# Order of the row groups and of the opening block pairs in the seven-product gated blocks

## The chip, the cores and the metric

The kernel runs on one core of one Trainium2 chip. The metric is the device time of one execution in microseconds. A profiled execution has a span (first to last instruction) and a total time slightly above it.

## The reference, cut to what matters

Two transformer blocks, one behind the other, over x of 512 tokens by 1024 features, in float32. The second has two layers, each with two gated feed-forward blocks, four in all:

```
D_MODEL = 1024; SEQ = 512; D_FF_2 = 2816
def swiglu(h, wg, wu, wd):
    return (jax.nn.silu(h @ wg) * (h @ wu)) @ wd
...
    h = modulated_norm(x, norm_g[l, 0], sh1, sc1)
    x = x + 0.5 * g1 * swiglu(h, ffn_wg[l, 0], ffn_wu[l, 0], ffn_wd[l, 0])
    ...   # attention with pooling (layer 0) or short convolution (layer 1)
    x = x + 0.5 * g3 * swiglu(h, ffn_wg[l, 1], ffn_wu[l, 1], ffn_wd[l, 1])
```

## The kernel before, in words

The five engines run five programs written by hand. Each has its own order, and semaphores tie them together; an engine never passes an instruction that waits. Every float32 operand is held as a rounded high part and a low remainder, and every product is three matmuls: high by high, high by low, low by high. ScalarE makes the high part of a piece of weights (a copy into a rounded type), VectorE the low part (raw minus high).

**Groups.** The 2816 hidden columns of a gated block are 22 chunks of 128. `GROUPS` (lines 92 to 96) divides them into 8, 8 and 6. For each group the kernel first makes the hidden rows, two chunks at a time (a block pair: two chunks of gate weights in raw slot 0, two chunks of up weights in raw slot 1, 1024 KB each, loaded by the SP queue), and then multiplies them by the group's rows of the down weights: four units of two output chunks, each unit a sum over the group's chunks (`down`). Behind a unit VectorE adds its result, times a gate, to the residual `xT` (`residual`, line 2359). The last group's last unit is `product_tail`: its second output chunk is made in two token halves, and after three k of the second half TensorE puts in the partial sums of the next norm. The norm's rstd and the first normed rows (ScalarE, line 1534) follow from these sums, and `first_products` (line 818) starts on them.

**Seven products.** In three of the four gated blocks (`SEVEN`; the fourth, layer 0's first, has plain products throughout) the two first pairs of group 0 are plain and all other pairs, nine in each block, are made by seven block products in place of eight: the weights and the activations are cut into 2 by 2 blocks, sums of blocks are multiplied, and the results are combined. This is done for gate (g) and up (u). The weight blocks come in seven batches:

- batch 1 (gate) and 2 (up): two blocks each, straight from the raw slots;
- sums made by VectorE in place, for each of g and u, in the order s3, s2, s4, s1 (`block_sum`, line 2917, 128x512 each; s2 is written into `stats`);
- batch 3: the two s2 sums; batch 4 and 5: s3 and s1 of gate and of up; batch 6 and 7: the rest of gate and of up. The low part of batch 6 frees raw slot 0 and that of batch 7 raw slot 1 for the next load.

`block_hi` (ScalarE, line 1913) and `block_lo` (VectorE, line 2893) split a batch. Batches 4, 5 and 6 live in `x_hi`/`x_lo`, the others in `w_hi`/`w_lo`. TensorE multiplies in the order p1g, p2g, p1u, p2u, p6g, (batch 4), p6u, p7g, (batch 5), p7u, p4g, (batch 6), p4u, (batch 7): 14 block products of 12 matmuls 128x256 (`block_product`, lines 1121 to 1123). p1g of the next pair waits for silu21, p1u for mul21, and p4u for u3u:

```
                else:
                    pe.wait_ge(s_y_act, y_act.after("silu21", w - 1))
                block_product(first_bank(0), 1, 0, *b11, start=True).then_inc(s_y_pe, y_pe.one("p1g"))
...
                else:
                    pe.wait_ge(s_y_dve, y_dve.after("mul21", w - 1))
                block_product(first_bank(1), 2, 0, *b11, start=True).then_inc(s_y_pe, y_pe.one("p1u"))
...
                pe.wait_ge(s_y_act, y_act.after("u3u", w))
                block_product(first_bank(1), 7, 1, *t4).then_inc(s_y_pe, y_pe.one("p4u"))
```

**Taking a pair's results.** `seven_taken` exists for ScalarE and for VectorE. ScalarE copies partial results out of the accumulators (`kept`, line 1955: u1g, u1u, u2g, u2u, u3g, u3u), takes the silus (lines 1986, 1992, 1996) and, between them, splits the batches of the next pair (`ahead`). VectorE adds the blocks: first block (line 2995), fourth block (line 3001, which needs u3), second block (line 3007), then the products mul21 (line 3056), mul22 and mul1; between them it makes the next pair's low parts (`lo`) and sums (`total`).

**Heads.** The first seven-product pair of a group is its head; the head of group 0 (pair 2) is the opening pair. The batches of a head are made ahead by `opening_blocks` and `seven_group`. For a later group this happens in the residual of the down product before it: behind the third unit (v == 2) batch 1, the sums, batches 2, 4, 6; behind the fourth (v == 3) batch 3. Before the change a later head has its four up sums there too, and its batches 5 and 7 stand ahead on ScalarE and just behind first block g on VectorE; the opening pair makes s4u, s1u and batches 5 and 7 inside `seven_taken`. p1g and p1u of a head wait for the residual updates of the units before (`out_taken`).

Of the kernel before, what the change touches and what calls it, by code (L numbers as in the profile page):

```python
# [51 lines left out]
def hybrid_two_block_kernel(  # L52
# [37 lines left out]
    u = U_FF + 8 * FFG  # L90

    GROUPS = []
    left = FF2 // P
    while left:
        GROUPS.append(min(8, left))
        left -= GROUPS[-1]
    U_FFN = {}
    U_AB = U_ABO = U_C = U_CO = 0
    for l in range(2):
        for j in range(2):  # L100
            if j == 1:
                if l == 0:
                    U_AB, U_ABO, u = u, u + 8, u + 12
# [24 lines left out]
    with ctx:  # L128
# [1363 lines left out]
        def _(act):  # L1492
# [448 lines left out]
            def seven_taken(l, j, g, i):  # L1941

                un = U_FFN[l, j, g] + 2 * i
                w = SEVEN_FIRST[l, j, g] + i
                head = i == seven_from(l, j, g)
                opening = head and g == 0
                more = i + 1 < GROUPS[g] // 2

                def ahead(batch):
                    if more:  # L1950
                        block_hi(batch, l, j, g, i + 1)

                def kept(step, s, q, after):
                    act.wait_ge(s_y_pe, y_pe.after(after, w))
                    act.activation(ev[:, 1, q * QT:(q + 1) * QT], first_bank(s), ACT.Copy)\  # L1955
                        .then_inc(s_y_act, y_act.one(step))

                if not head:
                    act.wait_ge(s_y_dve, y_dve.after("c12g", w - 1))
                kept("u1g", 0, 0, "p1g")  # L1960
                if not head:
                    act.wait_ge(s_y_dve, y_dve.after("mul1", w - 1))
                    hidden_hi(l, j, g, i - 1)
                    act.wait_ge(s_y_dve, y_dve.after("c12u", w - 1))
                elif g == 0:
                    act.wait_ge(out_taken[1], un + 2)
                    hidden_hi(l, j, g, i - 1)
                kept("u1u", 1, 2, "p1u")
                if opening:
                    block_hi(5, l, j, g, i)  # L1970
                    block_hi(7, l, j, g, i)
                ahead(1)
                kept("u2g", 0, 0, "p6g")
                if not head:
                    ahead(2)
                kept("u2u", 1, 2, "p6u")
                kept("u3g", 0, 1, "p7g")
                if head:
                    ahead(2)
                if not more:  # L1980
                    next_hi(un + 2, 0)
                ahead(3)
                kept("u3u", 1, 3, "p7u")
                ahead(4)
                act.wait_ge(s_y_pe, y_pe.after("p4g", w))
                act.activation(ev[:, 0, 2 * QT:3 * QT], first_bank(0), ACT.Silu).then_inc(s_y_act, y_act.one("silu21"))
                ahead(5)
                ahead(6)
                if not more:
                    next_hi(un + 3, 1, (0,))  # L1990
                act.wait_ge(s_y_dve, y_dve.after("c22g", w))
                act.activation(ev[:, 0, 3 * QT:4 * QT], ev[:, 0, 3 * QT:4 * QT], ACT.Silu)\
                    .then_inc(s_y_act, y_act.one("silu22"))
                ahead(7)
                act.wait_ge(s_y_dve, y_dve.after("c12g", w))
                act.activation(ev[:, 0, 0:2 * QT], ev[:, 0, 0:2 * QT], ACT.Silu).then_inc(s_y_act, y_act.one("silu1"))
                if not more:
                    act.wait_ge(s_y_dve, y_dve.after("mul1", w))
                    hidden_hi(l, j, g, i)
                    act.wait_ge(chunk_done, 2 * un + 4)  # L2000
                    next_hi(un + 3, 1, (1,))
# [8 lines left out]
            def seven_group(l, j, g, n):  # L2010

                for i in range(seven_from(l, j, g)):
                    un = U_FFN[l, j, g] + 2 * i
                    done(un)
                    if i == 0:
                        weight_hi(un + 2, s=0)
                        act.wait_ge(s_t_dve, t_dve.after("r4", SEVEN.index((l, j))))
                    act.activation(ev[:, 0, :], po[:, 0, :, :].rearrange("p b n -> p (b n)"), ACT.Silu)\
                        .then_inc(out_taken[0], 2)
                    if i + 1 < PLAIN_PAIRS:  # L2020
                        if i:
                            weight_hi(un + 2, s=0)
                        weight_hi(un + 3, (0,), s=1)
                        act.wait_ge(out_taken[1], un + 4)
                        hidden_hi(l, j, g, i)
                        weight_hi(un + 3, (1,), s=1)
                        if i == 0:
                            sums_hi(l, j)
                        continue
                    for batch in (1, 2, 4, 6, 3):  # L2030
                        block_hi(batch, l, j, g, i + 1)
                    first_sum_hi(l, j)
                for i in range(seven_from(l, j, g), n // 2):
                    seven_taken(l, j, g, i)
                if g + 1 < len(GROUPS):
                    for v in range(2):
                        weight_hi(U_FFN[l, j, g] + n + v + 2, s=v % 2)
                    for batch in (1, 2, 4, 6, 5, 3, 7):
                        block_hi(batch, l, j, g + 1, 0)

            def ffn(l, j, before):
# [219 lines left out]
        def _(dve):  # L2261
# [638 lines left out]
            def block_sum(step, l, j, g, i):  # L2900

                w = SEVEN_FIRST[l, j, g] + i
                c = step[-1]
                s = "gu".index(c)
                if step[:2] == "s3":
                    dve.wait_ge(s_x_dve[s], x_dve[s].after("lo", w))
                    out_, a, b, op = raw_block(s, 0, 0), raw_block(s, 0, 0), raw_block(s, 1, 0), ALU.subtract
                elif step[:2] == "s2":
                    dve.wait_ge(s_x_sum, x_sum.after("s3" + c, w))
                    out_, a, b, op = sum_block(s), raw_block(s, 1, 1), raw_block(s, 0, 0), ALU.subtract  # L2910
                elif step[:2] == "s4":
                    dve.wait_ge(s_x_sum, x_sum.after("s2" + c, w))
                    out_, a, b, op = raw_block(s, 0, 1), raw_block(s, 0, 1), sum_block(s), ALU.subtract
                else:
                    dve.wait_ge(s_x_sum, x_sum.after("s3" + c, w))
                    out_, a, b, op = raw_block(s, 1, 0), raw_block(s, 1, 0), raw_block(s, 1, 1), ALU.add
                dve.tensor_tensor(out_, a, b, op).then_inc(s_x_sum, x_sum.one(step))  # L2917
# [45 lines left out]
            def first_sum_lo(l, j):  # L2963
                dve.wait_ge(s_t_act, t_act.after("hi1", SEVEN.index((l, j))))
                dve.tensor_tensor(a_lo[:, 0:4, H[1]], t1_raw, a_hi[:, 0:4, H[1]].bitcast(F32), ALU.subtract)\
                    .then_inc(s_t_dve, t_dve.one("lo1"))
# [7 lines left out]
            def seven_taken(l, j, g, i):  # L2974
# [39 lines left out]
                first_block("g", ev[:, 0, 0:QT])  # L3014
                if opening:
                    first_sum_lo(l, j)
                    block_sum("s4u", l, j, g, i)
                    block_sum("s1u", l, j, g, i)
                elif head:
                    block_lo(5, l, j, g, i)  # L3020
                    block_lo(7, l, j, g, i)
                if not head or g == 0:
                    hidden_lo(l, j, g, i - 1)
                dve.wait_ge(s_w_dve, ffn_dve[l, j, g].before(i))
                first_block("u", hid[:, 0:QT])
                if opening:
                    block_lo(5, l, j, g, i)
                    block_lo(7, l, j, g, i)
                lo(1)
# [3 lines left out]
                total("s1g")  # L3033
                if head:
                    fourth_block("g", ev[:, 0, 3 * QT:4 * QT])
                lo(2)
                total("s3u")
                total("s2u")
# [3 lines left out]
                total("s1u")  # L3042
                if not more:
                    weight_lo(un + 2, s=0)
                if not head:
                    lo(3)
                fourth_block("u", hid[:, 3 * QT:4 * QT])
                if head:
                    lo(3)
                lo(4)  # L3050
                lo(5)
                lo(6)
# [26 lines left out]
            def opening_blocks(l, j, g, i):  # L3079

                block_lo(1, l, j, g, i)
                for step in ("s3g", "s2g", "s4g", "s1g"):
                    block_sum(step, l, j, g, i)
                block_lo(2, l, j, g, i)
                block_lo(4, l, j, g, i)
                block_lo(6, l, j, g, i)
                for step in ("s3u", "s2u", "s4u", "s1u")[:2 if g == 0 else 4]:
                    block_sum(step, l, j, g, i)

            def blocks_ahead(v, l, j, g):  # L3090
# [322 lines left out]
```

## Time and profile before

| what | value |
|---|---|
| median of 3 runs | 2678.87 us (2678.52 to 2680.12) |
| profiled execution, time / span | 2677.81 us / 2676.0 us |
| TensorE busy | 2649.5 us (99%) |
| VectorE busy | 1762.3 us (66%) |
| ScalarE busy | 1082.7 us (40%) |
| moved by DMA | 324.33 MB, mean 121 GB/s |

PE is TensorE, DVE VectorE, ACT ScalarE. Busy shares are averages over the whole span. Instructions on one engine overlap a little, so the distance between two starts is often less than the duration in the row. The seven-product blocks lie between 1440 us and the end.

### The profile page before, as it was taken

To read this page: it belongs to the slowest core of one execution; us is meant where nothing else is said; L and a number is where in the kernel's file an instruction comes from. 1 tells how busy PE (TensorE), PEld (TensorE's weight loads), DVE (VectorE), ACT (ScalarE), POOL (GpSimd) and SP (SyncE) were. 2 spreads that over 40 slices of the span, in tenths; PEclk is the share of its full clock that TensorE was granted. 3 is DMA by queue.
4 is the path that set the end of the run, shared out by engine and by line. 5 is a ranking of instruction groups with operands and counts; after the bars stand their busy time and mean duration, and the time that the engine had idled before them with its cause. 6 is when DMAs were issued, how large, how long until landed. Compare 5 with 4: busy or idle time off the path is not lost.

```text
span 2676.0 us, 37108 instructions
## 1 busy us (share of the span) xinstructions
PE 2649.5 (99%) x14953; PEld 2317.5 (87%) x14953; DVE 1762.3 (66%) x2177; ACT 1082.7 (40%) x1497; POOL 71.2 (3%) x119
## 2 busy tenths in 40 slices
PE   8999999999999999999999999999999999999999
PEld 7888988888888888888878899988899988888998
DVE  7677563586666765667567776867676654676775
ACT  5555432332223422224465434445343432453433
POOL 1000000000000000000400000000000000000000
PEclk9999999999999999999999999999999999999999
DMA  4111232555565365654212233323233222232322
GB/s 144 63 63 63 74 100 94 183 201 200 200 205 193 132 206 196 216 192 141 81 48 95 95 95 111 98 92 97 93 111 110 95 95 95 85 105 83 122 95 79
DMA packets 257930, 324.33 MB, mean 121 GB/s; under 512 B 5767, under 2 KB 248709, under 8 KB 249605
## 3 DMA queue, kind: packets, MB, share of 16 engines
q1 hardware_dynamic: 245904, 245.12, 28.6%
q0 software_dynamic: 9216, 75.50, 7.6%
q10 hardware_dynamic: 2676, 1.84, 0.2%
q8 instruction: 95, 1.56, 0.2%
q14 instruction: 39, 0.31, 0.0%
HBM read 320.34 MB, written 2.10 MB: 120 GB/s over the span
## 4 chain that ended last, share of the span: by engine, by line
PE 95%; DVE 2%; DMA 1%; ACT 1%; issue 0%; ACTq 0%; DVEq 0%; SPq 0%
PE po L749 18%; PE po L751 18%; PE po L750 17%; PE po L1121 5%; PE po L1123 5%; PE po L1122 5%; PE po L919 2%; PE pm L949 2%; PE po L921 2%; PE po L920 1%; PE po L818 1%; PE po L820 1%; PE po L833 1%; PE po L866 1%; PE po L852 1%; PE po L861 1%
## 5 line engine op out<-in xcount | busy, mean ns | idle before, releaser
L1504 ACT ACTIVATE w_hi<-w_raw 128x1024 fp32r<-128x1024 f32 x326 | 329.6, 1050 | 567.7 <-PE po L751 529.7
L2270 DVE TENSOR_TENSOR w_lo<-w_raw,w_hi 128x1024 fp32r<-128x1024 f32 x364 | 432.7, 1220 | 176.5 <-ACT w_hi L1504 171.0
L749 PE MATMUL po<-b_hi,w_hi 128*128 128x512 f32 x1008 | 392.8, 390 | 0.0
L750 PE MATMUL po<-b_lo,w_hi 128*128 128x512 f32 x1008 | 392.2, 389 | 0.0
L751 PE MATMUL po<-b_hi,w_lo 128*128 128x512 f32 x1008 | 392.2, 389 | 0.0
L749 PE MATMUL po<-a_hi,w_hi 128*128 128x512 f32 x976 | 380.1, 389 | 0.0
L751 PE MATMUL po<-a_hi,w_lo 128*128 128x512 f32 x976 | 379.7, 389 | 0.0
L750 PE MATMUL po<-a_lo,w_hi 128*128 128x512 f32 x976 | 379.7, 389 | 0.0
L751 PEld LDWEIGHTS po<-b_hi,w_lo 128*128 128x128 f32 x1008 | 189.2, 188 | 39.3
L750 PEld LDWEIGHTS po<-b_lo,w_hi 128*128 128x128 f32 x1008 | 189.3, 188 | 39.0
L749 PEld LDWEIGHTS po<-b_hi,w_hi 128*128 128x128 f32 x1008 | 189.3, 188 | 38.8
L750 PEld LDWEIGHTS po<-a_lo,w_hi 128*128 128x128 f32 x976 | 183.2, 188 | 38.0
L751 PEld LDWEIGHTS po<-a_hi,w_lo 128*128 128x128 f32 x976 | 183.2, 188 | 38.0
L749 PEld LDWEIGHTS po<-a_hi,w_hi 128*128 128x128 f32 x976 | 183.2, 188 | 37.8
L2359 DVE SCALAR_TENSOR_TENSOR xT<-po,gate,xT 128x512 f32<-128x512 f32 x104 | 74.1, 734 | 184.7 <-PE po L751 175.4
L2719 DVE SCALAR_TENSOR_TENSOR ada_acc<-ada_in,c_act,ada_acc 128x2304 f32<-128x2304 f32 x56 | 146.2, 2611 | 0.0
L1913 ACT ACTIVATE w_hi<-w_raw 128x1024 fp32r<-128x1024 f32 x81 | 84.3, 1055 | 96.5 <-PE po L751 53.2
L2893 DVE TENSOR_TENSOR w_lo<-w_raw,w_hi 128x1024 fp32r<-128x1024 f32 x81 | 98.5, 1219 | 31.3 <-ACT w_hi L1913 31.3
L1913 ACT ACTIVATE x_hi<-w_raw 128x1024 fp32r<-128x1024 f32 x81 | 82.6, 1055 | 56.1 <-DVE w_raw L2917 56.1
L1121 PE MATMUL po<-t_hi,w_hi 128*128 128x256 f32 x324 | 92.3, 285 | 8.9 <-ACT ev L1955 8.9
L1955 ACT ACTIVATE ev<-po 128x256 f32<-128x256 f32 x162 | 60.1, 374 | 96.9 <-PE po L1123 96.7
L2893 DVE TENSOR_TENSOR x_lo<-w_raw,x_hi 128x1024 fp32r<-128x1024 f32 x81 | 95.0, 1218 | 0.0
(473 smaller groups left out, 5727.4 us busy)
## 6 DMA issues: line engine op xcount, KB each, us to landing
ada_in<-in_w_ada_dram POOLq DMA_DIRECT2D x64, 1152.0 KB, 5.5
w_raw<-in_ffn_wg_dram SPq DMA_DIRECT2D x44, 1024.0 KB, 5.4
w_raw<-in_ffn_wu_dram SPq DMA_DIRECT2D x44, 1024.0 KB, 5.3
w_raw<-in_w_ff_dram SPq DMA_DIRECT2D x32, 1024.0 KB, 5.3
w_raw<-in_ffn_wd_dram SPq DMA_DIRECT2D x32, 1024.0 KB, 5.0
w_raw<-in_w_in_dram SPq DMA_DIRECT2D x27, 1024.0 KB, 5.1
w_raw<-in_ffn_wd_dram SPq DMA_DIRECT2D x16, 768.0 KB, 4.3
w_raw<-in_w_in_c_dram SPq DMA_DIRECT2D x12, 1024.0 KB, 5.1
```

What stands on the lines that cost most here:

```text
L749: pe.matmul(o, wh, hi[:, k, :], start=(k == ks[0]), stop=False)
L750: pe.matmul(o, wh, lo[:, k, :], start=False, stop=False)
L751: mm = pe.matmul(o, wl, hi[:, k, :], start=False, stop=(k == ks[-1]))
L1121: pe.matmul(o, wh[:, c], hi[:, k, :], start=(start and k == 0), stop=False, skip_group_check=True)
L1122: pe.matmul(o, wh[:, c], lo[:, k, :], start=False, stop=False, skip_group_check=True)
L1123: mm = pe.matmul(o, wl[:, c], hi[:, k, :], start=False, stop=(k == 3), skip_group_check=True)
L1504: act.activation(w_hi[:, s, part], w_raw[:, s, part], ACT.Copy).then_inc(hi_done, 1)
L1913: ins = act.activation(batch_out(ring_hi(batch), batch), batch_raw(batch), ACT.Copy)
L2270: dve.tensor_tensor(w_lo[:, s, part], w_raw[:, s, part], w_hi[:, s, part].bitcast(F32), ALU.subtract).then_inc(lo_done, 1)
L2359: return dve.scalar_tensor_tensor(xT[:, c, cols_], got, gates[:, c:c + 1], xT[:, c, cols_], ALU.mult, ALU.add)
L2719: ins = dve.scalar_tensor_tensor(ada_acc[:, :], ada_in[:, k % 2, :], c_act[:, k:k + 1], ada_acc[:, :], ALU.mult, ALU.add)
L2893: ins = dve.tensor_tensor(batch_out(ring_lo(batch), batch), batch_raw(batch), batch_out(ring_hi(batch), batch).bitcast(F32), ALU.subtract)
```

## The change

The last group is moved into second place, so the groups are 8, 6, 8 in all four gated blocks. Every head is now made in the order of the opening pair: s4u, s1u and batches 5 and 7 move into `seven_taken`. In every head, the opening ones too, ScalarE copies u3u ahead of the next pair's batches 2 and 3, and VectorE's fourth block of u stands ahead of the next pair's low part 2.

```
@@ GROUPS
         GROUPS.append(min(8, left))
         left -= GROUPS[-1]
+    GROUPS.insert(1, GROUPS.pop())
@@ ScalarE, seven_taken
-                opening = head and g == 0
...
-                if opening:
+                if head:
                     block_hi(5, l, j, g, i)
                     block_hi(7, l, j, g, i)
                 ahead(1)
...
                 kept("u3g", 0, 1, "p7g")
-                if head:
-                    ahead(2)
                 if not more:
                     next_hi(un + 2, 0)
-                ahead(3)
-                kept("u3u", 1, 3, "p7u")
+                if head:
+                    kept("u3u", 1, 3, "p7u")
+                    ahead(2)
+                    ahead(3)
+                else:
+                    ahead(3)
+                    kept("u3u", 1, 3, "p7u")
                 ahead(4)
@@ ScalarE, seven_group
-                    for batch in (1, 2, 4, 6, 5, 3, 7):
+                    for batch in (1, 2, 4, 6, 3):
                         block_hi(batch, l, j, g + 1, 0)
@@ VectorE, seven_taken
                 if opening:
                     first_sum_lo(l, j)
+                if head:
                     block_sum("s4u", l, j, g, i)
                     block_sum("s1u", l, j, g, i)
-                elif head:
-                    block_lo(5, l, j, g, i)
-                    block_lo(7, l, j, g, i)
...
                 first_block("u", hid[:, 0:QT])
-                if opening:
+                if head:
                     block_lo(5, l, j, g, i)
                     block_lo(7, l, j, g, i)
                 lo(1)
...
                 if head:
                     fourth_block("g", ev[:, 0, 3 * QT:4 * QT])
+                    fourth_block("u", hid[:, 3 * QT:4 * QT])
                 lo(2)
...
+                lo(3)
                 if not head:
-                    lo(3)
-                fourth_block("u", hid[:, 3 * QT:4 * QT])
-                if head:
-                    lo(3)
+                    fourth_block("u", hid[:, 3 * QT:4 * QT])
                 lo(4)
@@ VectorE, opening_blocks
-                for step in ("s3u", "s2u", "s4u", "s1u")[:2 if g == 0 else 4]:
+                for step in ("s3u", "s2u"):
                     block_sum(step, l, j, g, i)
```

## Rows read from the trace of the kernel before

**Rows 1.** The page: busy time, and the chain that ended last by engine.
```profile
PE 2649.5 (99%) x14953; PEld 2317.5 (87%) x14953; DVE 1762.3 (66%) x2177; ACT 1082.7 (40%) x1497; POOL 71.2 (3%) x119
...
PE 95%; DVE 2%; DMA 1%; ACT 1%; issue 0%; ACTq 0%; DVEq 0%; SPq 0%
```
**Rows 2.** Waits of TensorE: total us, times, longest.
```profile
PE po L1121 <- ACT ev L1955: 8.9, 3, 3.0
```
**Rows 3.** Timeline of TensorE (start, us): starts of seven-product pairs, and around them.
```profile
1480.49 0.28 PE L1121 MATMUL po<-a_hi,w_hi 128*128 128x256 f32 x1
...
1566.84 0.39 PE L749 MATMUL po<-b_hi,w_hi 128*128 128x512 f32 x1
...
1567.52 0.28 PE L1121 MATMUL po<-a_hi,w_hi 128*128 128x256 f32 x1
...
1587.72 0.28 PE L1121 MATMUL po<-a_hi,w_hi 128*128 128x256 f32 x1
...
1919.70 0.28 PE L1121 MATMUL po<-a_hi,w_hi 128*128 128x256 f32 x1
...
1940.06 0.28 PE L1121 MATMUL po<-a_hi,w_hi 128*128 128x256 f32 x1
```
**Rows 4.** The chain of work inside the first opening pair: start, us, what.
```profile
1490.31 5.25 DMA w_raw<-in_ffn_wu_dram
...
1495.58 1.07 ACT w_hi L1913
...
1496.68 1.24 DVE w_lo L2893
...
1500.35 0.38 ACT ev L1955
...
1500.86 0.36 PE po L1121
```
**Rows 5.** Timelines of ScalarE and VectorE in that pair.
```profile
1492.20 0.38 ACT L1955 ACTIVATE ev<-po 128x256 f32<-128x256 f32 x1 [1.06 <-PE po L1123]
...
1500.61 1.05 ACT L1913 ACTIVATE x_hi<-w_raw 128x1024 fp32r<-128x1024 f32 x1
...
1483.66 0.42 DVE L2995 TENSOR_TENSOR ev<-ev,pm 128x256 f32<-128x256 f32 x1 [0.56 <-PE pm L1123]
...
1500.00 0.68 DVE L2917 TENSOR_TENSOR w_raw<-w_raw 128x512 f32<-128x512 f32 x1
...
1501.09 1.22 DVE L2893 TENSOR_TENSOR w_lo<-stats,w_hi 128x1024 fp32r<-128x1024 f32 x1
...
1505.96 0.41 DVE L3056 TENSOR_TENSOR hid<-ev,po 128x256 f32<-128x256 f32 x1
```
**Rows 6.** The same in group 1's head of the first seven-product block.
```profile
1572.95 1.22 DVE L2893 TENSOR_TENSOR w_lo<-w_raw,w_hi 128x1024 fp32r<-128x1024 f32 x1
...
1579.51 1.05 ACT L1913 ACTIVATE w_hi<-w_raw 128x1024 fp32r<-128x1024 f32 x1
...
1589.88 0.41 DVE L3056 TENSOR_TENSOR hid<-ev,po 128x256 f32<-128x256 f32 x1
```
**Rows 7.** Timeline of VectorE in the down product ahead of that head.
```profile
1557.99 1.22 DVE L2893 TENSOR_TENSOR w_lo<-w_raw,w_hi 128x1024 fp32r<-128x1024 f32 x1 [0.35 <-ACT w_hi L1913]
...
1566.12 0.69 DVE L2917 TENSOR_TENSOR stats<-w_raw 128x512 f32<-128x512 f32 x1
...
1568.06 1.40 DVE L2359 SCALAR_TENSOR_TENSOR xT<-po,gate,xT 128x512 f32<-128x512 f32 x2
```
**Rows 8.** TensorE at a norm, behind a six-chunk and an eight-chunk tail.
```profile
1787.76 0.35 PE L818 MATMUL po<-a_hi,w_hi 128*128 128x256 f32 x1 [0.66 <-ACT a_hi L1534]
...
2317.03 0.36 PE L818 MATMUL po<-a_hi,w_hi 128*128 128x256 f32 x1
```
**Rows 9.** TensorE by stretches: length, busy, granted clock, DMA share, GB/s.
```profile
2384.00:2387.20 3.20, 3.20 (x17) 0.50 0.02 5
...
1500.80:1504.00 3.20, 3.14 (x26) 1.00 0.02 5
```

More of the change, by code:

```diff
@@ L96, in hybrid_two_block_kernel @@
         left -= GROUPS[-1]
+    GROUPS.insert(1, GROUPS.pop())
     U_FFN = {}
@@ L1945, in seven_taken @@
                 head = i == seven_from(l, j, g)
-                opening = head and g == 0
                 more = i + 1 < GROUPS[g] // 2
@@ L1968, in seven_taken @@
                 kept("u1u", 1, 2, "p1u")
-                if opening:
+                if head:
                     block_hi(5, l, j, g, i)
@@ L1977, in seven_taken @@
                 kept("u3g", 0, 1, "p7g")
-                if head:
-                    ahead(2)
                 if not more:
                     next_hi(un + 2, 0)
-                ahead(3)
-                kept("u3u", 1, 3, "p7u")
+                if head:
+                    kept("u3u", 1, 3, "p7u")
+                    ahead(2)
+                    ahead(3)
+                else:
+                    ahead(3)
+                    kept("u3u", 1, 3, "p7u")
                 ahead(4)
@@ L2037, in seven_group @@
                         weight_hi(U_FFN[l, j, g] + n + v + 2, s=v % 2)
-                    for batch in (1, 2, 4, 6, 5, 3, 7):
+                    for batch in (1, 2, 4, 6, 3):
                         block_hi(batch, l, j, g + 1, 0)
@@ L3016, in seven_taken @@
                     first_sum_lo(l, j)
+                if head:
                     block_sum("s4u", l, j, g, i)
                     block_sum("s1u", l, j, g, i)
-                elif head:
-                    block_lo(5, l, j, g, i)
-                    block_lo(7, l, j, g, i)
                 if not head or g == 0:
@@ L3025, in seven_taken @@
                 first_block("u", hid[:, 0:QT])
-                if opening:
+                if head:
                     block_lo(5, l, j, g, i)
@@ L3035, in seven_taken @@
                     fourth_block("g", ev[:, 0, 3 * QT:4 * QT])
+                    fourth_block("u", hid[:, 3 * QT:4 * QT])
                 lo(2)
@@ L3044, in seven_taken @@
                     weight_lo(un + 2, s=0)
+                lo(3)
                 if not head:
[L3046 to L3049, printed above, removed]
+                    fourth_block("u", hid[:, 3 * QT:4 * QT])
                 lo(4)
@@ L3086, in opening_blocks @@
                 block_lo(6, l, j, g, i)
-                for step in ("s3u", "s2u", "s4u", "s1u")[:2 if g == 0 else 4]:
+                for step in ("s3u", "s2u"):
                     block_sum(step, l, j, g, i)
```

## The prediction

> **What bounds the kernel now.** I read the page first: TensorE is busy for 99% of the span and the chain that ended last runs on it for 95% [rows 1]. So the busy shares decide nothing here; the change can only act where TensorE stands still. The list of its waits comes next. In the gated blocks with seven products the only large ones are three, of 3.0 us each, 8.9 us in all, ended by ScalarE's copy on line 1955 [rows 2]. Then the chain inside such a wait and the timelines of the engines around it, for the opening pair (block pair 2 of group 0) and for the pair that opens a later group. The reader is to see in them which instruction sits behind which on each engine, and how much room it has.
>
> I write T for the start of a pair's first matmul: 1480.49 for an opening pair, 1567.52 for a later head [rows 3]. A pair is 14 block products of 12 matmuls. Group 1's head takes 20.20 us to the next pair at 1587.72, with 0.04 of waiting in it [rows 3]: 0.12 us a matmul, 1.44 a product, 20.16 a pair. p1g starts at T, p1u at T+2.88, p6g at T+5.76, p7u at T+12.96, p4u at T+17.28, the next pair's p1u at T+23.04.
>
> **The opening pairs.** In the chain VectorE's split of batch 7 frees the second raw buffer at 1490.3, the next up weights land 5.25 us later, ScalarE splits batch 2 at 1495.58, VectorE makes its low part at 1496.68 and then the sum s2u, and only then come ScalarE's batch 3 and its copy u3u (1500.35), for which TensorE's p4u (1500.86) has waited, 2.94 us [rows 2, 4]. The change puts u3u ahead of batches 2 and 3. p7u's result is there at T+14.59 (u3g ran at 1492.20 = T+11.71, and p7u is two products later [rows 5]), so u3u runs at 1495.1 in time that ScalarE now waits for the transfer, and p4u starts on time.
>
> But what is late next? The next pair's p1g waits for silu21 and its p1u for mul21, and these stand behind batches 3 and 4 on ScalarE and behind the low parts 3, 4, 5, 6 on VectorE. Those still hang on the same transfer. VectorE's sum s1u starts at 1500.00 and lasts 0.68, which the next instruction overlaps by some 0.08 when it is ready; low part 3 then starts at 1500.60, not at 1501.09, because the fourth-block sum between them has moved ahead; from low part 3 to mul21 it is 4.87 us (1501.09 to 1505.96), mul21 takes 0.41 and I add 0.05 for the signal [rows 5]. So p1u starts at 1500.60+5.33 = 1505.93 = T+25.44. Before, p1u started at 1500.86+0.07+5.76 = 1506.69 = T+26.20 (four products after the wait). The gain is 0.76 us a pair, 2.3 us for three, not 9. TensorE's idle time becomes about 1.1 us ahead of p1g (batch 4 now follows batch 3 directly, silu21 at 1501.3) and 1.3 us ahead of p1u.
>
> **The heads of later groups (six: two in each of three blocks).** Before, their batches 5 and 7 and the sums s4u and s1u are made ahead, during the down products; batch 7's low part starts at 1572.95, ends 6.6 us after T, and ScalarE's batch 2 runs at 1579.51 = T+11.99 [rows 6]. mul21 starts at 1589.88 and ends at 1590.29; the next pair starts at 1587.72, so p1u needs it at 1590.60 [rows 3, 6]: room of 0.3 us. After, VectorE does first sum g at T+3.17 (as 1483.66 shows), the two sums (0.60 each, as s1u) [rows 5], first sum u at T+6.05 (p2u is two products behind p2g), low part 5 at 6.39, low part 7 from 7.53 to 8.75. The transfer lands at T+14.0. ScalarE, however, now holds batch 2 behind u3u, until T+14.59+0.26 = T+14.85 (1500.35 to 1500.61 is that 0.26 [rows 4, 5]). From batch 2 on, the opening pair's own distances hold: low part 2 after 1.10 (1495.58 to 1496.68 [rows 4]), low part 3 after 3.92 more (1496.68 to 1500.60), p1u after 5.33 more. That is T+25.20 against 1590.60 = T+23.08: 2.12 us later per head, 12.7 for six. From it comes what heads already lose before, at p4u: the worst next pair starts 1940.06-1919.70 = 20.36 after its head, 0.20 over 20.16, that of group 1 in the first block 0.04 [rows 3]; both are already in the start that I compare with, so the others give back at most 0.16 each. I take 0.4 in all: +12.3. Queued behind batch 2 on ScalarE are batches 3 and 4 and silu21, and TensorE waits for all of them; the SP queue's up-weight load moves 2.1 us later (from T+6.6 to T+8.75) but lands before ScalarE can use it. The bounds: if ScalarE could take batch 2 as it lands (T+14.05), a head costs 1.3 us, 7.9 in all; if low part 7 came 1 us later than worked out, 0.25 more each.
>
> **Groups 8, 6, 8.** The number of block pairs, matmuls and seven-product pairs is the same, and so are the ScalarE and VectorE instructions of the plain block. Two things move. First, the last group's down product now has eight chunks. Its last half-chunk has three k left after the norm's partial sum with six chunks, five with eight; those 6 matmuls (0.72 us) run where TensorE now waits 0.66 us for the first normed rows (1787.76), while the eight-chunk tail shows no wait there (2317.03) [rows 8]. Three ends: -2.1 us. Second, the head of group 2 now follows a six-chunk down product, whose units last 36 matmuls of 0.2267 us (1566.84 to 1567.52 is three [rows 3]), 8.16 us in place of 10.88. The low part 1 starts at T-9.53 and the second sum (1566.12) ends at 1566.84 [rows 7]; with the shorter unit this is T-6.81 to T+2.04, and the last two residual updates (1.40 for both [rows 7]) end at T+3.45. The two sums that the change takes out of this stretch are already left out in that. p1u at T+2.88 waits for these updates: 0.65 us, three heads, +2.0.
>
> **The clock.** The granted clock is 0.50 from 2384.00 to 2387.20, after the third of the 3 us waits, and there matmuls cost 1.5 us extra; after the other two it stays at 1.00, as 1500.80 to 1504.00 shows for the first [rows 9]. The new waits, 2.2 to 2.4 us within four at nine places, might bring as many falls or none: from -1.5 to +12. I take one such stretch as before, so nothing.
>
> The Trainium skill (TensorE: Matmul & The Clock Gate, Part 1) says that activity releases the throttle and idling brings the lower level back. By that rule waits half as long with matmuls between them keep the full rate, and the sum would be 1.5 us lower.
>
> The Trainium skill (DMA: Bandwidth & Descriptors, Anatomy of one DMA) gives, for the software path, 2.0 us plus bytes over 436 GB/s; an estimate by it is 4.4 us for these 1024 KB. This case's chain shows 5.25 [rows 4], and the measurement decides; by the page the opening pairs would gain 0.2 us more each, and the later heads nothing, since ScalarE is not free sooner.
>
> **Sum.** -2.3+12.3+2.0-2.1 = +9.9 us. The profiled execution took 2677.81 us (span 2676.0 and 1.8 around it) and would take 2687.7; the median before is 2678.87, 1.1 us above it, so I forecast 2688.8. What a measurement of this kernel can tell from no change is about 0.2%, 5.4 us.
>
> **Rivals.** (A) *The three waits go and nothing takes their place*: the openings give 3 x 3.16 = 9.5, the clock 1.5, the heads 0.4, the ends 2.1, group 2 takes 2.0: 2667.4. It needs mul21 before T+23.04. Against it: before, mul21 ended at T+25.9 in the opening pair, and only 0.5 us leaves its queue; for it: VectorE is busy 66% [rows 1], so its queue might be filled otherwise than I read. It decides for the faster side once the new places cost less than 0.2 us a head. Chance 0.10. (B) *The later heads cost 0.8 to 1.3 us*, because batch 2 is bound by its transfer or the low parts run in less time: +5, 2683.9, no difference. Chance 0.12. (C) *The clock falls at most of the nine places*, 1.5 us each: +9, 2697.8. For it speaks the one fall in three, against it that each wait is under half as long. Chance 0.12. The forecast itself: 0.66, its own range 2685 to 2692.
>
> The range takes in B and the lower falls of C: 2682 to 2694. Faster 0.10 (A), within 0.2% 0.13 (B and a little), slower 0.77.
>
> **What would show it.** In the profile after: no wait at p4u of the opening pairs; waits in front of the first and third product of the pair behind each head, nine of each, ended by silu21 (line 1986) and mul21 (line 3056), about 0.9 and 1.3 us; ScalarE's batch 2 of later heads at T+14.85; group 2's p1u waiting 0.6 us for the residual; no wait of 0.7 before the norm's first product. It is wrong if batch 2 runs near T+12 in later heads, or if mul21 stands before T+23.

## The result, and the profile after

The changed kernel takes 2687.92 us (median of 7 runs, 2686.98 to 2689.31) against 2678.89 us for the kernel before on the same chips; the ratio is 1.0035, 95% interval [1.0024, 1.0045]. It is slower, by 9.0 us; forecast were 9.9 and a median of 2688.8. The profiled execution has a span of 2686.1 us, 10.1 more than before. Its time, 2687.90 us, is the median of the changed kernel, while that of the kernel before lay 1.1 us under its median; the forecast carried these 1.1 us over to the changed kernel.

The page of the changed kernel: busy time, and the chain that ended last by engine. Line numbers have moved by one (1121 is now 1122) and, further down, by three.

```profile
span 2686.1 us, 37156 instructions
...
PE 2652.3 (99%) x14977; PEld 2318.4 (86%) x14977; DVE 1762.4 (66%) x2177; ACT 1083.0 (40%) x1497; POOL 71.4 (3%) x119
...
PE 92%; DVE 5%; ACT 1%; DMA 1%; issue 1%; ACTq 0%; DVEq 0%
```

VectorE and ScalarE do the same work as in [rows 1], and in the same time; yet VectorE's share of the chain has gone from 2% to 5%. Nothing was added: the work hangs together differently. The list of TensorE's waits names where (total us, times, longest):

```profile
PE po L1122 <- DVE hid L3056: 10.1, 9, 1.1
PE po L1122 <- ACT ev L1989: 8.2, 9, 1.3
...
PE po L1122 <- DVE xT L2362: 1.4, 3, 0.5
```

The three waits of 3.0 us in [rows 2] are gone, and so are the three of 0.7 us for the norm's first rows. In their place stand nine for silu21 (line 1989), nine for mul21 (line 3056) and three for the residual. An idle time in these rows is some 0.16 us smaller than the time lost, because a matmul's row lasts 0.28 us while the next one starts 0.12 us after it.

TensorE's timeline in the first seven-product block: the start of the opening pair, then p1g and p1u of the pair behind it; the head of group 1 with the same two; then p1u of group 2's head. These answer to [rows 3].

```profile
1479.21 0.28 PE L1122 MATMUL po<-a_hi,w_hi 128*128 128x256 f32 x1
...
1500.51 0.36 PE L1122 MATMUL po<-a_hi,w_hi 128*128 128x256 f32 x1 [0.99 <-ACT ev L1989]
...
1504.73 0.35 PE L1122 MATMUL po<-a_hi,w_hi 128*128 128x256 f32 x1 [1.11 <-DVE hid L3056]
...
1565.63 0.28 PE L1122 MATMUL po<-a_hi,w_hi 128*128 128x256 f32 x1
...
1586.71 0.35 PE L1122 MATMUL po<-a_hi,w_hi 128*128 128x256 f32 x1 [0.78 <-ACT ev L1989]
...
1590.93 0.35 PE L1122 MATMUL po<-a_hi,w_hi 128*128 128x256 f32 x1 [1.11 <-DVE hid L3056]
...
1665.10 0.36 PE L1122 MATMUL po<-a_hi,w_hi 128*128 128x256 f32 x1 [0.45 <-DVE xT L2362]
```

ScalarE and VectorE in group 1's head, T = 1565.63 (answers to [rows 6]): u3u and batch 2 right behind it, batch 3, silu21; then VectorE's first sum u, low part 5, the low parts 7 and 1, low part 3, mul21.

```profile
1580.22 0.38 ACT L1955 ACTIVATE ev<-po 128x256 f32<-128x256 f32 x1 [2.50 <-PE po L1124]
1580.50 1.05 ACT L1914 ACTIVATE w_hi<-w_raw 128x1024 fp32r<-128x1024 f32 x1
1584.30 1.06 ACT L1914 ACTIVATE w_hi<-stats 128x1024 fp32r<-128x1024 f32 x1 [2.74 <-DVE stats L2920]
...
1586.21 0.36 ACT L1989 ACTIVATE ev<-po 128x256 f32<-128x256 f32 x1
...
1571.68 0.42 DVE L2998 TENSOR_TENSOR hid<-ev,pm 128x256 f32<-128x256 f32 x1 [1.26 <-PE pm L1124]
1572.02 1.22 DVE L2896 TENSOR_TENSOR x_lo<-w_raw,x_hi 128x1024 fp32r<-128x1024 f32 x1
1573.15 2.35 DVE L2896 TENSOR_TENSOR w_lo<-w_raw,w_hi 128x1024 fp32r<-128x1024 f32 x2
...
1585.51 1.22 DVE L2896 TENSOR_TENSOR w_lo<-stats,w_hi 128x1024 fp32r<-128x1024 f32 x1
...
1590.38 0.41 DVE L3056 TENSOR_TENSOR hid<-ev,po 128x256 f32<-128x256 f32 x1
```

The reader is to see ScalarE idle for 2.50 us in front of the copy u3u and batch 2 starting 0.28 us behind it. The row of batch 2 names no transfer as its releaser, where the chain of before had one in the opening pair [rows 4]: in this trace the up weights are issued at 1574.40 and have landed at 1579.91, 0.59 us before batch 2, and the copy, which waits for TensorE, stood in front of them.

### The profile page after: what moved, and what is told of

Its sections match the earlier page's. It is cut to its first block, busy times and chain, and to the rows that moved or that the text cites. A ratio compares the mean times of both kernels' runs of the same rounds, so it can differ in the third digit from the quotient of the medians.

```text
span 2686.1 us, 37156 instructions
## 1 busy us (share of the span) xinstructions
PE 2652.3 (99%) x14977; PEld 2318.4 (86%) x14977; DVE 1762.4 (66%) x2177; ACT 1083.0 (40%) x1497; POOL 71.4 (3%) x119
## 3 DMA queue, kind: packets, MB, share of 16 engines
q10 hardware_dynamic: 2676, 1.84, 0.2%
## 4 chain that ended last, share of the span: by engine, by line
PE 92%; DVE 5%; ACT 1%; DMA 1%; issue 1%; ACTq 0%; DVEq 0%
PE po L750 17%; PE po L752 17%; PE po L751 17%; PE po L1122 5%; PE po L1124 4%; PE po L1123 4%; PE po L920 2%; PE pm L950 2%; PE po L922 2%; PE po L921 1%; PE po L819 1%; DVE w_lo L2896 1%; DVE x_lo L2896 1%; PE po L821 1%; DVE w_raw L2920 1%; PE po L834 1%
## 5 line engine op out<-in xcount | busy, mean ns | idle before, releaser
L750 PE MATMUL po<-b_hi,w_hi 128*128 128x512 f32 x992 | 386.5, 390 | 0.0
L751 PE MATMUL po<-b_lo,w_hi 128*128 128x512 f32 x992 | 386.0, 389 | 0.0
L752 PE MATMUL po<-b_hi,w_lo 128*128 128x512 f32 x992 | 386.0, 389 | 0.0
L1122 PE MATMUL po<-a_hi,w_hi 128*128 128x256 f32 x324 | 93.1, 287 | 19.6 <-DVE hid L3056 10.1
```

Source lines behind the costliest of these rows:

```text
L750: pe.matmul(o, wh, hi[:, k, :], start=(k == ks[0]), stop=False)
L751: pe.matmul(o, wh, lo[:, k, :], start=False, stop=False)
L752: mm = pe.matmul(o, wl, hi[:, k, :], start=False, stop=(k == ks[-1]))
L1122: pe.matmul(o, wh[:, c], hi[:, k, :], start=(start and k == 0), stop=False, skip_group_check=True)
```

## The experiments

Each run stands beside runs of the kernel before on its own chip, so the ratios are to be compared, not the medians from different chips. "Queue theory" is the name in the expectations for my account: the heads are slow because of what stands ahead of batch 2, silu21 and mul21 on their engines.

**e1: the order of the groups alone.**

```
 before.py
+    GROUPS.insert(1, GROUPS.pop())
```

> The kernel before with groups 8, 6, 8 and nothing else. Queue theory (a transfer, a split or a sum is late because of what stands ahead of it on its engine): three tails save 0.7 us each; the head of group 2 now follows a six-chunk down product with all four up sums still ahead of the residual updates, so its p1u waits until T+4.65 in place of T+2.88, 1.8 us three times; +3.4 us against before, about 2682.3, and a wait of TensorE for the residual (line 2360) of 1.6 to 1.8 us three times. The three 3.0 us waits at p4u of the opening pairs stay. Rival (the order of the groups has no price of its own): only the tails change, -2.1 us, 2676.8.

Measured: 2687.07 us (2684.37 to 2691.74, 8 runs), ratio 1.0026 [1.0015, 1.0036]; 4.8 us above my number, of which 1.3 are in the runs of the kernel before too (2680.19 us here), and by itself nearly as slow as the whole change. TensorE's waits, and stretches of its timeline (length, busy, granted clock, DMA share, GB/s), two behind p4u of opening pairs and two behind p1u of group 2's heads:

```profile
PE po L1122 <- ACT ev L1956: 9.6, 4, 3.0
PE po L1122 <- DVE xT L2360: 5.3, 3, 1.8
```
```profile
1500.60:1503.70 3.10, 3.10 (x16) 0.50 0.00 0
1855.60:1858.60 3.00, 3.00 (x16) 0.50 0.02 5
2022.90:2025.90 3.00, 3.00 (x16) 0.50 0.00 0
2555.40:2558.40 3.00, 3.00 (x16) 0.50 0.00 0
1665.80:1670.00 4.20, 4.20 (x35) 1.00 0.16 54
```

The residual wait is there as worked out, 1.8 us three times, and the tails are right. What I had not put a price on is the clock: in this execution it falls four times, against once in the profiled execution of before [rows 9], behind two of the three waits of 3.0 us and behind two of the three of 1.8. Each costs 1.5 us. Three more falls are 4.5 us, and a wait of 0.66 us at p4u of one of group 2's heads (the fourth in the first row) makes the rest: 6.0 for the residual with its slow restarts, 0.8, 4.5, less 2.1 for the tails, is 9.2; the span grew by 9.1. That sum compares the two profiled executions. So the order of the groups has a price of its own, and the rival falls. In the whole change the new order of the heads takes s4u and s1u out of this stretch and shortens these waits to 0.45 us.

**e2: the order of the heads alone** (the whole change, groups 8, 8, 6).

```
 after.py
-    GROUPS.insert(1, GROUPS.pop())
```

> The whole change without the order of the groups (8, 8, 6 as before). Queue theory: the opening pairs gain 3 x 0.6, the six later heads lose 2.4 each less 0.7 that they lost before; the group order is worth -2.1 and +2.1, so this kernel is as slow as the whole change, 2687 to 2689, with waits in front of p1g (0.8 to 1.3 us) and p1u (1.1) behind each of the nine heads, and with no residual wait, but with the 0.7 us waits at the norms. Rival (the six-chunk group in the middle is what costs): 2680 or less.

Measured: 2688.54 us, ratio 1.0031 [1.002, 1.0043]. As the queue theory has it: the same nine and nine waits, no residual wait, and the norm's three waits back.

```profile
PE po L1121 <- DVE hid L3055: 10.1, 9, 1.1
PE po L1121 <- ACT ev L1988: 8.3, 9, 1.2
...
PE po L818 <- ACT a_hi L1534: 2.0, 3, 0.7
```

With the new heads the group order is worth nothing either way, 2.1 gained at the tails and 2.0 lost at the heads of group 2.

**e3: u3u and the fourth block of u first, nothing else.** Batches 5 and 7 of later heads stay ahead.

```
 before.py, ScalarE
-                if head:
-                    ahead(2)
                 if not more:
                     next_hi(un + 2, 0)
-                ahead(3)
-                kept("u3u", 1, 3, "p7u")
+                if head:
+                    kept("u3u", 1, 3, "p7u")
+                    ahead(2)
+                    ahead(3)
+                else:
+                    ahead(3)
+                    kept("u3u", 1, 3, "p7u")
 VectorE: fourth_block("u") ahead of lo(2) in heads, as in the change
```

> The kernel before with only the order of u3u and the fourth block of u changed in every head; batches 5 and 7 and all sums of later heads stay made ahead. Queue theory: in later heads ScalarE's batch 2 moves from T+12.0 to T+14.9 because it stands behind u3u, whatever the transfer does; silu21 and mul21 come as late as in the whole change: 2.2 to 2.4 us per later head, about 2687 to 2689. Rival (late-buffer theory: the later heads lose because their batch 7 is split late and frees raw slot 1 2.1 us later): no loss here, the openings gain 1.9 us and the clock may give 1.5: 2675.5 to 2677.

Measured: 2688.67 us, ratio 1.0029 [1.0018, 1.0041]. The waits are those of e2 to 0.1 us in total. ScalarE in group 1's head, T = 1566.11:

```profile
1580.70 0.38 ACT L1955 ACTIVATE ev<-po 128x256 f32<-128x256 f32 x1 [2.50 <-PE po L1123]
1580.98 1.05 ACT L1913 ACTIVATE w_hi<-w_raw 128x1024 fp32r<-128x1024 f32 x1
```

VectorE's fourth block of u and low part 2 there:

```profile
1581.12 0.42 DVE L3004 TENSOR_TENSOR hid<-ev,po 128x256 f32<-128x256 f32 x1 [2.46 <-ACT ev L1955]
1582.06 1.22 DVE L2896 TENSOR_TENSOR w_lo<-w_raw,w_hi 128x1024 fp32r<-128x1024 f32 x1 [0.53 <-ACT w_hi L1913]
```

Batch 2 starts at T+14.87, as in the whole change (1580.50-1565.63 = 14.87), although here the raw slot was freed as early as before: the load is issued at T+6.69 and has landed at T+11.9. The run also moves a VectorE instruction, the fourth block of u; the two rows show that it costs nothing here, since VectorE is done with it and idle for 0.53 us when batch 2's high part comes. So moving one copy of 0.4 us ahead of batches 2 and 3 costs as much as the whole new order of the heads. The late-buffer theory falls as the only explanation of the change; that a late buffer costs nothing does not follow, and e4 and e8 look at that.

**e4: batches 5 and 7 and the two sums late, nothing else.** u3u and the fourth block stay where they were; groups 8, 8, 6.

```
 before.py, ScalarE
-                if opening:
+                if head:
                     block_hi(5, l, j, g, i)
                     block_hi(7, l, j, g, i)
...
-                    for batch in (1, 2, 4, 6, 5, 3, 7):
+                    for batch in (1, 2, 4, 6, 3):
 VectorE
+                if head:
                     block_sum("s4u", l, j, g, i)
                     block_sum("s1u", l, j, g, i)
-                elif head:
-                    block_lo(5, l, j, g, i)
-                    block_lo(7, l, j, g, i)
...
                 first_block("u", hid[:, 0:QT])
-                if opening:
+                if head:
                     block_lo(5, l, j, g, i)
                     block_lo(7, l, j, g, i)
...
-                for step in ("s3u", "s2u", "s4u", "s1u")[:2 if g == 0 else 4]:
+                for step in ("s3u", "s2u"):
```

> The kernel before with only s4u, s1u and batches 5 and 7 of later heads moved into the head; u3u and the fourth block of u where they were. Queue theory: the up transfer lands at T+14.1, ScalarE takes batch 2 at once, and u3u behind batch 3 comes at about T+18.9: TensorE waits at p4u, about 2.1 us in each of six later heads beside the three 3.0 us waits of the openings: +12 us, 2690 to 2692. Rival (the two causes add, each worth half of the whole): 1.2 us per later head, +6.5, 2685.

Measured: 2698.8 us, ratio 1.0064 [1.0048, 1.0081], the slowest of all. The waits of TensorE; ScalarE in group 1's head (T = 1568.40) with batch 2, batch 3 and u3u; TensorE's p4u there; and a stretch behind p4u of the second block's opening pair (2.16 us busy of 4.00, granted clock 0.65); then the load of up weights in the last head of the third block, and a stretch at the third block's opening pair:

```profile
PE po L1121 <- ACT ev L1954: 22.4, 9, 3.3
```
```profile
1582.39 1.06 ACT L1913 ACTIVATE w_hi<-w_raw 128x1024 fp32r<-128x1024 f32 x1 [1.90 <-DMA w_raw<-in_ffn_wu_dram]
1586.20 1.06 ACT L1913 ACTIVATE w_hi<-stats 128x1024 fp32r<-128x1024 f32 x1 [2.75 <-DVE stats L2916]
1587.16 0.37 ACT L1954 ACTIVATE ev<-po 128x256 f32<-128x256 f32 x1
```
```profile
1587.67 0.36 PE L1121 MATMUL po<-t_hi,w_hi 128*128 128x256 f32 x1 [1.84 <-ACT ev L1954]
```
```profile
1857.50:1861.50 4.00, 2.16 (x10) 0.65 0.00 0
```
```profile
2600.93 6.50 DMA w_raw<-in_ffn_wu_dram
```
```profile
2395.00:2401.00 6.00, 5.48 (x26) 0.50 0.01 3
```

The transfer now is the releaser of batch 2, at T+13.99 (expected T+14.1), and p4u waits 1.84 to 3.3 us in every head. The two causes do not add. Where the clock holds, a later head loses 2.2 to 2.3 us here, 2.3 in e3, and 2.3 to 2.4 with both, because both delay the same instruction, batch 2 (T+14.0 to T+14.2 in these heads, T+14.87 in e3). What the expectation missed, 7 to 9 us, lies again with the clock: in the profiled execution it falls at six of the nine waits, once for twice as long as at the others (the last row lies in that fall). The rest is one later head that waits 3.14 us, because its load took 6.50 us, and the 1.3 us by which the kernel before is slower in these runs.

**e5: the new order in the three opening pairs only** (e3's edits under `opening` in place of `head`).

```
 before.py, ScalarE
-                if head:
+                if head and not opening:
                     ahead(2)
                 if not more:
                     next_hi(un + 2, 0)
-                ahead(3)
-                kept("u3u", 1, 3, "p7u")
+                if opening:
+                    kept("u3u", 1, 3, "p7u")
+                    ahead(2)
+                    ahead(3)
+                else:
+                    ahead(3)
+                    kept("u3u", 1, 3, "p7u")
 VectorE: fourth_block("u") ahead of lo(2) if opening
```

> The kernel before with the new order of u3u and of the fourth block of u in the three opening pairs only; later heads and groups as before. Queue theory: the 3.2 us at p4u become 1.2 us ahead of p1g and 1.35 ahead of p1u, 0.6 us gained each, 1.9 us; waits this short have brought no fall of the clock in the whole change, so the 1.5 us that such a fall costs go too: 2674 to 2676. Rival (the three waits are simply removed): 2678.9 - 9.6 - 1.5 = 2668.

Measured: 2674.09 us, ratio 0.9977 [0.9968, 0.9986]. The granted clock of the span is 1.00.

```profile
PE po L1121 <- ACT ev L1991: 3.6, 3, 1.2
PE po L1121 <- DVE hid L3064: 3.3, 3, 1.1
```

The waits did not go, they were cut up and moved; the rival, 2668, falls. The part of the change that meets the 3.0 us waits is faster than before by 6 us on its own chip. TensorE's time at the three pairs gives 1.3 of them. The rest fits the clock: all 11 executions of this kernel have a mean granted clock of 1.000, and the 20 of the kernel before beside them 0.997 to 0.999, the slower ones the lower values. That is more loss than the one fall in the profiled execution of before, which took 2677.81 us against a median of 2680.78 here.

**e6: batch 7 earlier in the opening pairs**, the cause of the 3.0 us itself.

```
 before.py, ScalarE
-                kept("u1u", 1, 2, "p1u")
                 if opening:
                     block_hi(5, l, j, g, i)
+                kept("u1u", 1, 2, "p1u")
+                if opening:
                     block_hi(7, l, j, g, i)
 VectorE
-                first_block("g", ev[:, 0, 0:QT])
                 if opening:
-                    first_sum_lo(l, j)
                     block_sum("s4u", l, j, g, i)
                     block_sum("s1u", l, j, g, i)
+                first_block("g", ev[:, 0, 0:QT])
+                if opening:
+                    first_sum_lo(l, j)
+                    block_lo(5, l, j, g, i)
+                    block_lo(7, l, j, g, i)
...
                 first_block("u", hid[:, 0:QT])
-                if opening:
-                    block_lo(5, l, j, g, i)
-                    block_lo(7, l, j, g, i)
```

> The kernel before, and in the opening pairs alone s4u and s1u ahead of first block g, batch 5 ahead of the copy u1u, and the low parts 5 and 7 ahead of the older pair's hidden low part, so that batch 7's low part ends near T+7.6 in place of T+9.8 and the up transfer starts 2.2 us earlier. No order of u3u is touched. Queue theory: the wait at p4u shrinks by as much, from 3.2 to about 1 us, first sum u is about 0.5 us late for p6u: 1.7 to 2.5 us gained per opening pair, 5 to 7.5, and the clock's 1.5: 2670 to 2673. Rival (the wait at p4u comes from the order on ScalarE, not from the raw buffer): 2678.9, no change.

Measured: 2669.47 us, ratio 0.9958 [0.9945, 0.9972], 0.5 us under the range expected. ScalarE's batch 2 in the first opening pair, and TensorE's p4u:

```profile
1492.62 1.06 ACT L1913 ACTIVATE w_hi<-w_raw 128x1024 fp32r<-128x1024 f32 x1 [0.27 <-DMA w_raw<-in_ffn_wu_dram]
```
```profile
1497.90 0.35 PE L1121 MATMUL po<-t_hi,w_hi 128*128 128x256 f32 x1 [0.21 <-ACT ev L1955]
```

2.94 us of waiting have become 0.21, and 0.4 at p6u; each opening pair gives back 2.1 us. The up weights are issued at T+7.58, 2.24 us sooner than before. The wait came from the raw buffer; the order on ScalarE can stay.

**e7: e6, and u3u between batch 2 and batch 3 in every head.**

```
 the kernel of e6, ScalarE
                 if head:
                     ahead(2)
+                    kept("u3u", 1, 3, "p7u")
                 if not more:
                     next_hi(un + 2, 0)
                 ahead(3)
-                kept("u3u", 1, 3, "p7u")
+                if not head:
+                    kept("u3u", 1, 3, "p7u")
```

> The one before (e6), and on ScalarE u3u between batch 2 and batch 3 in every head. Queue theory: batch 2 keeps its place right behind its transfer, so nothing of silu21 and mul21 is later, and the waits at p4u go in all nine heads: 0.7 us for the later ones and up to 1 us for each opening, 2668 to 2671. Rival (copying u3u ahead of batch 3 costs as much as ahead of batch 2): 2682 or more.

Measured: 2668.21 us, ratio 0.9954 [0.994, 0.9967], the fastest. All waits at p4u are gone; what TensorE waits for in these blocks is first sum u, 0.4 us at p6u of the openings, and 0.4 once:

```profile
PE po L1121 <- DVE hid L2998: 1.2, 3, 0.4
...
PE po L1121 <- DVE ev L3004: 0.4, 1, 0.4
```

Here u3u passes batch 3 alone, and fits into the 2.7 us in which ScalarE waits in front of batch 3 for a VectorE sum anyway. The medians of e6 and e7, taken on one chip, differ by 1.3 us for the better, and each of e7's five runs (up to 2669.06) lies below each of e6's (from 2669.43).

**e8: the whole change with u3u behind batch 2** (and the fourth block of u behind low part 2).

```
 after.py, ScalarE
+                if head:
+                    ahead(2)
+                    kept("u3u", 1, 3, "p7u")
                 if not more:
                     next_hi(un + 2, 0)
-                if head:
-                    kept("u3u", 1, 3, "p7u")
-                    ahead(2)
-                    ahead(3)
-                else:
-                    ahead(3)
+                ahead(3)
+                if not head:
                     kept("u3u", 1, 3, "p7u")
```

> The whole change with u3u behind batch 2 in all heads and the fourth block of u behind low part 2. Batch 2 of later heads can then be taken as the transfer lands, T+14.1 in place of T+14.9: it measures how much of their 2.4 us is the late raw buffer alone. Queue theory: 0.5 us less in each of six later heads, 0.3 more in each opening: 2685.5 to 2686.5 against 2687.9. Rival (ScalarE's order alone is the cause and the late buffer costs nothing): 2675.

Measured: 2686.78 us, ratio 1.0022 [1.0012, 1.0031], with transfers in the chain as in the row below (group 1's head, issued 8.8 us after its start):

```profile
PE po L1122 <- DVE hid L3056: 10.1, 9, 1.1
PE po L1122 <- ACT ev L1988: 6.6, 9, 1.4
```
```profile
1574.76 5.82 DMA w_raw<-in_ffn_wu_dram
```

1.1 us less than the whole change by medians from different sets of runs, 1.6 less waiting: the waits for silu21 shrink, those for mul21 stay. A later head still loses 2.0 us on average, against 2.3 in the change, although its copy no longer stands in front of batch 2. The late raw buffer is thus enough for most of the loss, and the rival, 2675, falls. The gain is less than the 1.5 to 2.4 expected for two reasons. Batch 2 is bound by its transfer now, and the loads of the later heads took 5.26 to 5.98 us where I had counted 5.25. And the fourth block of u, behind low part 2, now stands ahead of the sums: from low part 2 to low part 3 it is 4.13 us (1581.70 to 1585.83) against 3.93 in the change (1581.58 to 1585.51), 0.2 us in each of nine heads.

## Why the prediction was right, point by point

- **Opening pairs: forecast -2.3, measured -1.4 (the clock has its own point).** In the first block p1u of the next pair starts at 1504.73 = T+25.52, forecast T+25.44. From a head's start to the next pair's start the three take 21.30, 21.61 and 21.47 us, and 1.4 more each are lost at p1u. The prediction took all three as alike, with a load of 5.25 us; in this trace the three loads take 5.24, 5.54 and 5.41 us, and p1u comes later by just these differences. It also counts 0.07 us for TensorE's slow restart behind the old wait and nothing behind the new ones. The mechanism, that the wait returns in front of p1g and p1u, is shown by the page of the change and by e5.
- **Later heads: forecast +12.3, measured +13.3.** Batch 2 starts at T+14.87 (forecast 14.85), low part 3 at T+19.88 (19.87), mul21 at T+24.75 (24.74). The six heads lose 2.33 to 2.41 us each, 14.07 in all, and gave back 0.73, not the 0.4 that I took. The term was undersized mainly by what a restart costs: behind each wait the second matmul starts 0.19 us after the first, not 0.12, and the signal from mul21 took 0.14 us (1590.38+0.41 to 1590.93), not 0.05. That u3u's place alone costs all of this is shown by e3; that the late batches alone would have cost nearly as much, by e4, and by e8 with 2.0 us a head.
- **Group 2's head behind six chunks: forecast +2.0, measured 0.67, 0.67, 0.66.** The two residual updates start at 1663.55, 1.93 us after the head's start at 1661.62, and take 1.40; forecast was T+2.04. e1 shows what they would have been with the sums ahead.
- **Tails: forecast -2.1.** The norm's waits are gone in e1 and in the change and there in e2, three of 0.66 us and a little.
- **Clock: forecast as before, one fall; measured none.** The step that I left open came out 1.5 us better. The other executions bear it out: all of the change, e2, e3, e5 and e8, 42 with the same pair of waits, have a mean granted clock of 1.000, while the 37 of the kernel before that stand beside the experiments have 0.997 to 0.999. So the one fall that the forecast took for before is that of its profiled execution, and not that of every one. By the Trainium skill (TensorE: Matmul & The Clock Gate, Part 1), activity keeps the full rate; the change's waits of at most 1.3 us show no fall, which agrees. The falls behind waits of 1.8 us in e1 and e4, among matmuls on both sides, do not fit it as well, and the measurement decides. A stretch of the change with 1.0 us of waiting in it:

```profile
1497.00:1502.00 5.00, 4.01 (x34) 1.00 0.00 0
```

- **Sum.** Openings, clock, later heads, group 2, tails: -1.4-1.5+13.3+2.0-2.1 = +10.3 us; the span grew by 10.1. The forecast's 9.9 is near it partly by luck, because errors cancel: the later heads lost 1.0 more than forecast and the openings gained 0.9 less, while the clock gave back 1.5 that the forecast did not count on. By the medians the growth is 9.0, since the 1.1 us between profiled execution and median did not carry over.
- **Rivals.** A (the waits are simply removed) is refuted, for the openings by e5 and for the whole by the nine waits for mul21. B (0.8 to 1.3 us per later head) is refuted by 2.3. C (the clock falls at the new waits) did not happen in the change; the clock fell in e1 and e4, whose waits are longer.
- **What stays open:** what exactly makes the clock fall. At waits of 1.8 us or more it falls in some cases and not in others of the same length, and behind pairs of 0.8 to 1.3 and 1.1 us in none of the nine of the change. No kernel here separates the length of a wait from what surrounds it.

## What to carry to other kernels

When a wait ends in one long chain (buffer free, transfer, split, sum), find what the same chain feeds next before moving the waiter: here in the opening pairs some 3.2 us went at the copy, and the silu and the product behind it lost 2.6 to 2.9 again. Moving an instruction that waits for another engine ahead of one that is ready delays the ready one, and all behind it, by the wait: in e3's later heads batch 2 starts 2.9 us later than before, and TensorE loses 2.3. e3 and e5 differ only in the six later heads, by the place of one copy and of the VectorE block that uses it (1.0029 against 0.9977, some 14 us); put behind batch 2 (e7 against e6) the copy costs nothing. Mend the start of the chain before its end (e6: 11 us by the medians on its chip, 7.5 us between the two profiled spans), and give an order that suits one case (the opening pairs) only to that case.

## What the runs showed of the hardware that I had not expected

The granted clock falls to 0.50, 1.2 GHz, at some waits of only 1.8 us: in e1 behind two of three, and 1.5 us are lost in each fall, so that such a wait costs up to 3.5 us. In e4 it stays there once through a stretch of 6.0 us. Falls make the measurement wide as well: e1 ran from 2684.4 us (mean granted clock 0.998) to 2691.7 (0.996), e7, which has no wait over 0.4 us in these blocks, from 2667.9 to 2669.1, all at 1.000. And a load of 1024 KB from the same queue took 5.25 us in one chain, 5.82 in another and 6.50 in a third, where batch 2 started 1.1 us later than in the other heads of that run.
